# RWKV-7 loop: four array quarters in the chunk chain, copies on two engines, six merge units between its phases

## The reference

```python
def step(state, inp):
    r_t, w_t, k_t, v_t, a_t, b_t = inp
    sa = jnp.einsum('bhvk,bhk->bhv', state, a_t)
    state = state * w_t[:, :, None, :] + sa[..., None] * b_t[:, :, None, :] + v_t[..., None] * k_t[:, :, None, :]
    return state, jnp.einsum('bhvk,bhk->bhv', state, r_t)
```

## Time and profile before

| what | us |
|---|---|
| median of 3 runs | 2528.36 (2527.67 to 2539.57) |
| the profiled execution's own time | 2526.31 |
| its span | 2524.4 |
| PE busy | 2410.1 (95%) |
| DVE busy | 1050.1 (42%) |
| ACT busy | 959.8 (38%) |
| POOL busy | 1045.0 (41%) |

### The profile page before, as it was taken

How to read it: one execution, slowest core, us unless ns; L and a number is a source line. 1 busy time by engine, 2 the same in 40 slices (tenths; PEclk the granted TensorE clock), 3 DMA queues, 4 the chain that set the end, 5 groups by cost and what they waited for, 6 DMA issues and landing times.

```text
span 2524.4 us, 38784 instructions
## 1 busy us (share of the span) xinstructions
PE 2410.1 (95%) x13928; PEld 1953.1 (77%) x13928; DVE 1050.1 (42%) x1776; ACT 959.8 (38%) x1273; POOL 1045.0 (41%) x756
## 2 busy tenths in 40 slices
PE   8999998889999999999999799999999998999997
PEld 6877777767788888788887578787888775888885
DVE  3355464555555532322211856663333345322213
ACT  3244432233566643444422422223444523444321
POOL 4212230014445555555555533442433255455554
PEclk9899999989999999999999899999999998999998
DMA  4111120013232233222332212221222132223232
GB/s 171 58 42 38 46 71 16 3 42 110 82 100 99 92 101 107 92 95 96 100 100 100 96 59 76 84 78 65 76 82 78 64 100 67 85 98 100 93 107 83
DMA packets 56746, 205.24 MB, mean 81 GB/s; under 512 B 6828, under 2 KB 7596, under 8 KB 56268
## 3 DMA queue, kind: packets, MB, share of 16 engines
q1 hardware_dynamic: 55152, 196.45, 23.6%
q10 hardware_dynamic: 1504, 7.49, 0.8%
HBM read 201.81 MB, written 2.10 MB: 81 GB/s over the span
## 4 chain that ended last, share of the span: by engine, by line
PE 86%; DVE 9%; ACT 2%; issue 2%; POOL 0%; DMA 0%; DVEq 0%; ACTq 0%; SPq 0%
PE psum L379 84%; DVE rope_t L2245 2%; DVE qk_st L2244 1%; PE psum L554 1%; DVE rope_t L2237 1%; DVE qk_st L2247 1%; POOL x L364 0%; PE psum L978 0%; DVE psum L1615 0%; ACT w_hi L1117 0%; DVE inv L1934 0%; DVE o_acc L1778 0%; DVE rst L1615 0%; DVE soft_r L1773 0%; DVE tmp L2169 0%
## 5 line engine op out<-in xcount | busy, mean ns | idle before, releaser
L352 POOL TENSOR_TENSOR w_lo<-raw,w_hi 128x512 fp32r<-128x512 f32 x732 | 1014.6, 1407 | 1447.8 <-ACT w_hi L1117 1447.8
L379 PE MATMUL psum<-h_hi,w_hi 128*128 128x512 f32 x2192 | 890.6, 406 | 40.8 <-DVE h_lo L1621 26.0
L379 PE MATMUL psum<-h_lo,w_hi 128*128 128x512 f32 x2192 | 865.4, 395 | 0.0
L1117 ACT ACTIVATE w_hi<-raw 128x1024 fp32r<-128x1024 f32 x366 | 386.2, 1056 | 807.7 <-PE psum L379 796.8
L379 PE MATMUL psum<-h_hi,w_lo 128*128 128x512 f32 x2192 | 551.9, 391 | 0.0
L379 PEld LDWEIGHTS psum<-h_hi,w_hi 128*128 128x128 f32 x2192 | 419.0, 191 | 153.1 <-issue 54.2
L379 PEld LDWEIGHTS psum<-h_lo,w_hi 128*128 128x128 f32 x2192 | 419.5, 191 | 89.3 <-issue 6.9
L379 PEld LDWEIGHTS psum<-h_hi,w_lo 128*128 128x128 f32 x2192 | 412.8, 188 | 87.5 <-issue 1.4
L379 PE MATMUL psum<-hid_hi,w_hi 128*128 128x512 f32 x528 | 208.7, 395 | 0.0
L379 PE MATMUL psum<-hid_lo,w_hi 128*128 128x512 f32 x528 | 208.6, 395 | 0.0
L1599 DVE TENSOR_TENSOR tmp<-psum,rst 128x512 f32<-128x512 f32 x100 | 69.1, 691 | 319.5 <-PE psum L379 319.0
(11 more groups left out here) (391 smaller groups left out, 2533.5 us busy)
## 6 DMA issues: line engine op xcount, KB each, us to landing
raw<-in_w SPq DMA_DIRECT2D x366, 512.0 KB, 3.3
x<-in_x SPq DMA_DIRECT2D x4, 512.0 KB, 6.3
tmp<-in_cmp_w ACTq DMA_DIRECT2D x1, 2048.0 KB, 7.3
x<-in_x ACTq DMA_DIRECT2D x1, 2048.0 KB, 7.7
out_y<-x SPq DMA_DIRECT2D x8, 256.0 KB, 2.1
mask<-in_mask ACTq DMA_DIRECT2D x1, 1536.0 KB
masks<-in_masks ACTq DMA_DIRECT2D x1, 768.0 KB, 9.4
lora<-in_lora ACTq DMA_DIRECT2D x1, 512.0 KB, 3.7
```

What stands on the lines that cost most here:

```text
L352: pool.tensor_tensor(w_lo[:, g.slot, part], raw[:, g.slot, part], w_hi[:, g.slot, part].bitcast(F32), ALU.subtract).then_inc(sem("lo_ready ...
L379: return pe.matmul(out, lhsT, rhs, start=start, stop=stop)
L1117: act.activation(w_hi[:, g.slot], raw[:, g.slot], ACT.Copy).then_inc(sem("hi_ready"), 1)
```

## The change

- In the chain, for p = 1 only, source and result swap partition halves from phase to phase (`place`), so that the four matmuls of a phase (p and e) name four different quarters of the array. p = 0 has bank 7, p = 1 bank 6.
- `second` and `fourth` add the old inverse in PSUM by products with the identity; what leaves PSUM is a plain copy. ACT copies for p = 0, DVE for p = 1. `near` is a tile of its own; the identity is added to it by `late_power`.
- Merge units 20 to 25 run inside rounds 0 to 5, an eighth (three matmuls) behind each phase, into bank 5; `take_loop` takes them at the end of DVE's round. ACT makes one high part a round from round 1 on.
- `keys_of(2)` and `keys_of(3)` come before all four norms; `pair_ready(2)` and `(3)` run at the end of rounds 1 and 3. PE waits for one pair at a time. `key_part` has four tiles.
- The gate rows are cut in three parts, one behind the ninth unit of heads 0, 1 and 2; the exponential over them moves from head 1 to head 3.

The core of the diff (blank lines left out too):

```diff
-        inv = sb("inv", [128, 2, 2, 64], scope=rw)
         dd = sb("dd", [128, 2, 2, 2, 64], scope=rw)
-        de = sb("de", [128, 2, 2, 2, 64], scope=rw)
+        inv_pow = sb("inv_pow", [128, 2, 2, 2, 64], scope=rw)
+        inv = inv_pow[:, :, 0]
+        power4 = inv_pow[:, :, 1]
+        near = sb("near", [128, 2, 2, 64], scope=rw)
...
+        def place(p, e, turned):
+            return half(1 - e if p == 1 and turned else e)
+        LOOP_FIRST, LOOP_UNITS = 20, 6
...
+            merge_unit(19)
             for i in range(4):
-                merge_unit(19 + i)
...
-            for c in (23, 24, 25):
-                merge_unit(c)
+            pe.wait_ge(sem("lora_taken"), 4)
+            pe.wait_ge(sem("lora_g_taken"), 4)
...
+                if c == 0:
+                    pe.wait_ge(sem("prepared"), i + 1)
...
+            def chain_ready(r, phase):
+                if 8 * r + phase > 1:
+                    pe.wait_ge(sem("chain_ok0"), 8 * r + phase - 1)
+                    pe.wait_ge(sem("chain_ok1"), 8 * r + phase - 1)
...
+            def in_order():
+                for h in range(2):
+                    for p in range(2):
+                        for e in range(2):
+                            yield h, p, e
...
+            def term_of(p, rows, h):
+                return (p7, p6)[p][rows, 256 + 64 * h:320 + 64 * h]
...
             def square(n, late):
...
+                last = [None, None]
+                for a in range(2):
+                    for h, p, e in in_order():
+                        k, rows, to = (n + p) % 4, place(p, e, late), place(p, e, not late)
+                        if late:
+                            d, t = wm[k][rows, h, 128:192], near[rows, p, h]
+                        else:
+                            d, t = sc[k][rows, h, 256:320], sc[k][rows, h, 0:64]
+                        out = squares_of(p, to, h, a)
+                        last[p] = mm(out, t, d) if a == 0 else mm(out, d, t)
+                last[0].then_inc(sem("chain_mm0"), 1)
+                last[1].then_inc(sem("chain_mm1"), 1)
...
+            def second(n, late):
+                r = n // 2
+                chain_ready(r, 6 if late else 2)
+                pe.wait_ge(sem("inv_ready"), 2 * r + (2 if late else 1))
...
+                for h in range(2):
+                    for p in range(2):
                         for e in range(2):
-                            mm(bank_of(p)[half(e), h, 0], t[half(e), h], d[half(e), h])
+                            rows, to = place(p, e, not late), place(p, e, late)
+                            mm(term_of(p, to, h), dd[rows, p, h, 0], inv[rows, p, h], True, False)
...
+                    for p in range(2):
                         for e in range(2):
...
+                            rows, to = place(p, e, not late), place(p, e, late)
+                            mm(term_of(p, to, h), idd[rows], inv[rows, p, h], False, True)
+                    for p in range(2):
                         for e in range(2):
-                            mm(term_of(p, h, e), dd[half(e), p, h, 0], inv[half(e), p, h])
+                            rows, to = place(p, e, not late), place(p, e, late)
+                            last[p] = mm(power_of(p, to, h), dd[rows, p, h, 1], dd[rows, p, h, 0])
...
+            def fourth(n, late):
+                r = n // 2
+                chain_ready(r, 7 if late else 3)
...
+                    for p in range(2):
                         for e in range(2):
...
+                            rows = place(p, e, late)
+                            mm(term_of(p, rows, h), power4[rows, p, h], inv[rows, p, h], True, False)
+                    for p in range(2):
                         for e in range(2):
...
+                            rows = place(p, e, late)
+                            last[p] = mm(term_of(p, rows, h), idd[rows], inv[rows, p, h], False, True)
...
             def apply_near(n):
...
+                for h, p, e in in_order():
+                    rows, to = place(p, e, False), place(p, e, True)
+                    mm(power_of(p, to, h), wm[(n + p) % 4][rows, h, 128:192], inv[rows, p, h])
+                last = [None, None]
+                for h, p, e in in_order():
+                    rows, to = place(p, e, False), place(p, e, True)
+                    last[p] = mm((p7, p6)[p][to, 192 * h:192 * h + 192], inv[rows, p, h], wm[(n + p) % 4][rows, h])
...
             def apply_far(n):
...
+                for h, p, e in in_order():
+                    rows, to = place(p, e, True), place(p, e, False)
+                    last[p] = mm((p7, p6)[p][to, 192 * h:192 * h + 128], inv[rows, p, h],
+                                 wm[(n + p) % 4][rows, h, 0:128])
...
+            def merge_part(n, ks):
+                if n // 2 >= LOOP_UNITS:
+                    return
+                w = Index(A_UNITS + LOOP_FIRST + n // 2)
+                if ks[0] == 0:
+                    open_unit(w)
+                    pe.wait_ge(sem(f"freed{(w + -1).slot}"), (w + -1).half() + 1)
+                for k in ks:
+                    mm_hi(p5, w.slot, k, h_hi[:, k], h_lo[:, k], k == 0)
+                for k in ks:
+                    if k % 4 == 0:
+                        open_low(w, k // 4)
+                    last = mm_lo(p5, w.slot, k, h_hi[:, k], k == 7)
+                if ks[-1] == 7:
+                    last.then_inc(sem("unit_used"), 1)
...
                 square(n, False)
+                merge_part(n, [0])
                 if n:
                     state_step(2 * n - 4)
                 if more:
                     turn_chunk(n + 2)
                 second(n, False)
+                merge_part(n, [1])
...
                 apply_near(n)
+                merge_part(n, [3])
...
+            def chain_copy(dst, src, r, phase, done=True):
+                act.wait_ge(sem("chain_mm0"), 8 * r + phase)
+                ins = act.activation(dst, src, ACT.Copy)
+                if done:
+                    ins.then_inc(sem("chain_ok0"), 1)
...
+                chain_copy(inv0, p7[:, 256:384], r, 3)
+                chain_copy(near0, p7[:, 384:512], r, 4, False)
+                chain_copy(wm[n % 4].rearrange("p h n -> p (h n)"), p7[:, 0:384], r, 4)
+                if 1 <= r <= min(LOOP_UNITS, 6):
+                    high_part(Index(A_UNITS + LOOP_FIRST + 1 + r))
...
             take_merge(19)
+            keys_of(2)
+            keys_of(3)
+            for i in range(4):
+                pair_norm(i)
             pair_ready(0)
-            take_merge(20)
-            keys_of(2)
             pair_ready(1)
-            take_merge(21)
-            keys_of(3)
-            pair_ready(2)
-            take_merge(22)
-            pair_ready(3)
-            for c in (23, 24, 25):
-                take_merge(c)
...
+            def late_power(n):
+                dve.wait_ge(sem("chain_ok0"), 4 * n + 4)
+                dve.wait_ge(sem("chain_ok1"), 4 * n + 4)
+                dve.tensor_tensor(inv[:, 0], near[:, 0], eye, ALU.add)
+                for e in range(2):
+                    last = dve.tensor_tensor(inv[half(1 - e), 1], near[half(e), 1],
+                                             idd[half(e)].unsqueeze(1).to_broadcast([64, 2, 64]), ALU.add)
+                last.then_inc(sem("inv_ready"), 1)
+            def chain_copy(dst, src, n, phase, done=True):
+                dve.wait_ge(sem("chain_mm1"), 4 * n + phase)
+                ins = dve.tensor_copy(dst, src)
+                if done:
+                    ins.then_inc(sem("chain_ok1"), 1)
...
+            def take_loop(n):
+                w = Index(A_UNITS + LOOP_FIRST + n // 2)
+                if n // 2 < LOOP_UNITS:
+                    dve.wait_ge(sem("unit_used"), w.value(1))
+                    dve.tensor_tensor(zm[:, w.at - A_UNITS, 1:], p5, rst[:], ALU.mult)\
+                        .then_inc(sem(f"freed{w.slot}"), 1)
...
-                near_applied(n)
+                chain_copy(near1, p6[:, 384:512], n, 4, False)
+                chain_copy(wm[(n + 1) % 4].rearrange("p h n -> p (h n)"), p6[:, 0:384], n, 4)
+                late_power(n)
...
                 terms(n)
                 if more:
                     values(n + 3)
+                take_loop(n)
+                if n in (2, 6):
+                    pair_ready(2 + n // 6)
...
-                        if hh == 0 and c == 2:
-                            gate_sums()
-                        if hh == 0 and c == 3:
-                            gate_maxima()
                         if c == 7:
                             att_max(0)
+                        if c == 8 and hh < 3:
+                            (gate_sums, gate_maxima, gate_floor)[hh]()
```

More of the change, by code:

```diff
@@ L139, in build_program @@
         omm = sb("omm", [128, 20], scope=z1)
-        key_part = [zm[:, 26 + n, 0:T] for n in range(2)]
+        key_part = [zm[:, 26 + n, 0:T] for n in range(4)]
         mix_part = [zm[:, 28 + n, 0:T] for n in range(2)]
@@ L705, in square @@
```

(23 more changed lines are left out.)

155 lines of the change are left out of this document (62 added, 93 removed).

## The result

The changed kernel takes 2542.22 us (median of 5 runs, 2539.35 to 2543.32), the kernel before 2534.79 us in the same session; the ratio is 1.0042, 95% interval 1.0028 to 1.0055. By the ratio that is **+10.6 us (7 to 14)**, while the medians differ by 7.4, where the prediction had -8.7. The profiled execution has a span of 2540.2 us.

What follows compares the result with a forecast made beforehand. It took a loop round as TensorE issue steps (12.2 of 15.80 us) plus waits for PSUM copies and sums on ACT and DVE. -20.1+0.7+1.4+13.5-1.7+4.0-6.5 = -8.7 us gave 2519.5 us, range 2506 to 2534.

Steps and rivals of the forecast that it cites:

- (e): Ahead of the loop: first mask at 359.4 against 379.52, -20.1 us, with 12.6 us of DVE work now exposed.
- first mask to first terms: First mask to first square at half clock throughout, +0.7 us; then round 0 up to its terms, +1.4 us.
- (c): Merge parts in rounds 0 to 5: round 18.5 us against 15.8, five times +13.5; rounds 6 and 7 together -1.7.
- (d): Pair work of heads 2 and 3 inside the loop, after rounds 1 and 3: +2.0 us each, +4.0.
- (f): Mixing stage: gate rows leave head 0 for new places, -6.5 us (ends -7.1 and -3).
- rival 4: Ahead of the loop: half clock lasts through round 0 and more, or gate rows give nothing: +5 to +7, 2525; chance 0.10.
- rival 3: Chain: the four quarters don't run together; fours serialised into pairs cost +4.6 us a round, +37, 2556; chance 0.07.
- (a): Chain on four quarters of the array: 40 steps instead of 64, 2.8 us less PE work per round.
- (b): Chain copies on ACT and DVE: gaps not much shorter (0.81 us, about 0.67 for 128 columns), covered by merge parts.
- rival 2: Loop: DVE becomes the bound, 1 us in each of eight rounds and 2 in pair rounds, +10, 2530; chance 0.16.

Runs made afterwards that it cites:

- e4: Changed kernel with seven unneeded 512-column matmuls on TensorE in front of the wait for VectorE's take, rounds 1 to 5; ratio 1.0036 to the kernel before.
- e3: Changed kernel with VectorE's take of the finished merge unit put in front of a round's terms; ratio 1.0030 to the kernel before.
- e2: Changed kernel with the six merge units and all pair work back ahead of the loop; ratio 1.0001 to the kernel before.
- e5: e2 with both chunks' square copies on ScalarE; ratio 0.9980 to the kernel before.
- e1: Kernel before with only the gate rows moved; ratio 0.9974 to the kernel before.
- e7: Changed kernel with e3, e5, e6, the first power before the terms, and pair work of heads 2 and 3 spread over two rounds each; 2518.11 us.
- e6: e2 with one VectorE add replacing the second chunk's identity products in `fourth`; ratio 0.9991 to the kernel before.
- e8: e2 with e5, e6 and the next round's first power before the terms; 2522.06 us.

## Why the prediction was wrong, step by step

By the traces, changed against before:

| step | predicted | measured |
|---|---|---|
| (e) first mask | -20.1 | -20.9 |
| first mask to first terms (0.7 and 1.4) | +2.1 | +3.2 |
| (c), (d) five intervals of rounds | +17.5 | +35.9 |
| (c) rounds 6 and 7 | -1.7 | +3.4 |
| (f) head 0 | -6.5 | -7.1 |
| sum | -8.7 | +14.5 |

The spans differ by 15.8 us, of which 2.2 lie before the change; the runs say 10.6 (7 to 14). The table compares one execution of each. T0 is taken as the start of VectorE's first terms less 0.28 us, as in the prediction. Parts (e) and (f) came as forecast, so rival 4 is out. So is rival 3: the four quarters do run together, 0.115 us a group in the late `second`, where each bank is written from both row halves. The Trainium skill, TensorEngine Tiling, Restrictions and Gotchas, rules out that different row tiles use one PSUM bank simultaneously; the trace, with these groups of four in 0.115 us, speaks against it for disjoint halves of the partitions.

**What failed is part (c), the round of 18.5 us.** The wait was placed rightly (part 0 at T0+2.64, forecast 2.6). Rounds 3 and 5, at 22.2 us, are 3.7 us longer than that for three reasons, of which the first is absent in round 1 (20.74 us):
- *The clock after the wait, 1.5 us* (e4). I counted 1.8 us of standing and full speed behind it, though I had charged half speed behind a wait ahead of the loop. The stretch from 480 to 485 us has a mean granted clock of 0.78.
- *A part is 1.06 us, not 0.85*: 1.13 between groups less the group's own 0.115, and 0.05 at the first group behind it (495.49 to 495.77). Eight of them: 1.7 us. My upper bound was 1.0. I had one row for a switch, 0.34 us for the first step. Here every border costs: 0.23 us ahead of the part instead of 0.115, 0.34 for its first step, 0.33 for its last, 0.28 at the group behind.
- *(a) counted `fourth` as four quarters.* It runs in pairs: eight more steps a round, 0.94 us. The diff shows it (`rows` twice); my count "fourths 2x4" does not.

These give 4.1 us, less the 0.3 us of gaps that I had allowed and that are not there: 3.8 us against the 3.7 measured. In e3, where the clock stays full, 71 steps at 0.115, 0.94 and seven parts of 1.06 give 16.5 us from `second` to T0; the trace has 16.4.

**(a), fewer steps are not less time.** From `second` to T0, e2 takes 13.05 us, the kernel before 13.29. Twenty steps less should be 2.3 us. `fourth` gave 0.94 of them back, interleaving the chunks gave up the overlap of copies with products (seen in the far product, not tested by a run), and **(b)** put one copy behind VectorE's powers: e5 takes 0.5 to 0.7 us off its undisturbed rounds by moving it. That was rival 2 in kind, VectorE's queue, at 0.5 to 0.7 us instead of 1.

The same error is in rounds 6 and 7. `second` comes at T0+3.7 and T0+3.1, as forecast (3.6 and 3.1), but from there to the next T0 it is 14.1 and 14.4 us where I had 11.8. The 13.05 us of e2 are the chain's share of that. The other 1.0 and 1.3 us are not separated; round 7 has a mean granted clock of 0.90.

**(d)** cost 2.5 and 2.9 us (24.73 and 25.12 against 22.2) where 2.0 was forecast. The mechanism was right: in round 2 `second` comes at T0+6.25, forecast 6.2. What is above 2.0 lies behind `second`, where the clock stayed low for longer: the two pair rounds have a mean of 0.86, rounds 3 and 5 have 0.92.

The sign turned on (c). Of the 18.4 us by which the five intervals exceed the forecast, some 11 are the parts and `fourth` (2.2 us in each, as in round 1, where the clock was full) and 7 go with the low clock in four of them. Without both the sum would be about -4 us by the traces; without either one alone it would still be above zero.

## What to carry to other kernels

Work that fills TensorE's gaps has two prices that its matmuls do not show: a switch into and out of its tile shape each time, and a wait for its bank, which can be paid again in a lower clock (here 1.5 us in two of three plain rounds). Put no more of it into a loop than the gaps hold (four units here came out 6.6 us ahead of six, though their intervals overlap), take its result before anything that does not need to come first, and spread long pieces of VectorE work. Before counting fewer steps as time, ask what follows each phase: two chunks one behind the other may hide a copy that two interleaved chunks expose.

## What the hardware showed that was not expected

- Behind stands of only 1.70 and 1.64 us the groups of `second` were 0.21 us apart instead of 0.115; behind one of 1.73 us in round 1 they were not, nor with the stretch filled (e4).
- Some rounds of one and the same loop are 1.2 to 2.4 us longer than their neighbours. In e5 the round of 18.09 us has this row, a TensorE that waited for nothing that the profile shows:

```profile
472.80 0.33 PE L387 MATMUL psum<-tm,zm 64*64 64x64 f32 x2 [1.94 <-issue]
```

Such gaps fall at other places in other kernels. Between the first and the last terms they sum to 0 us in the kernel before, 1.2 in e1, 1.9 in the changed kernel and 1.1 in e7, but to 5.5 in e2, 6.0 in e5, 6.4 in e6 and 3.7 in e8. So the kernels with the new chain and no parts beside it have the most of them, and their totals hold this beside what their edits do. No run here tested the cause, and it stays open.
